# Experts' loads: overflow pairs in reverse order at the same places, and half of one weight set asked for earlier

## Chip, cores and metric

The kernel runs on one core of one Trainium2 chip. The metric is the device time of one execution in microseconds. The median of the timed runs is what counts; the trace comes from one further, profiled execution.

## What is computed

Two transformer blocks in float32 on 512 tokens of width 1024. All that this change touches is the last stage, a mixture of 32 experts, of which each token uses two:

```python
def _hierarchical_moe(xt, w_rg, b_rg, w_re, b_re, w_gate, w_up, w_down):
    ...
    expert_id = g_idx * EXPERTS_PER_GROUP + top_i
    ...
    for e in range(N_EXPERTS):
        he = jax.nn.silu(xt @ w_gate[e]) * (xt @ w_up[e])
        y = y + combine[:, e:e + 1] * (he @ w_down[e])
```

Each of an expert's three matrices (gate and up 1024 x 256, down 256 x 1024) is 1 MiB, that is 1.0486 MB. There are 512 x 2 = 1024 pairs of a token and an expert, so 1024 rows of 4 KiB are gathered for the experts and as many are scattered back.

## The kernel before

**Tiles.** The experts' stage runs over `NP = 24` tiles, numbered n in the order in which TensorE takes them. A tile holds 64 rows for each of two experts (z = 0 and 1). 16 tiles are "main": main tile m serves the first 64 rows of experts 2m and 2m + 1. The other 8, at the places `OVER_AT = (3, 4, 7, 8, 11, 14, 17, 20)`, are "overflow" pairs, for experts with more than 64 rows. The kernel counts at run time how many blocks of 64 rows beyond the first each expert needs, lists them by rising expert, and gives them the ranks 0, 1, 2 and so on. Overflow pair m serves the ranks m (z = 0) and m + 8 (z = 1). `TILE_PAIRS[n]` says which pair stands at place n. In `WROW` stands, for each rank, from which rows of the weights its loads are to read; for a rank that nobody has, the rows lie behind the end of the tensor. There `bounds_check` drops the row: the instruction is issued all the same, but moves no weights.

**Loads.** A main tile's six matrices are asked for on SyncE's queue (`load_gate_up`, L549 and L550, and `load_down`, L556), an overflow tile's on GpSimd (`over_gate_up` and `over_down`, both through `over_rows`, L749). Gate and up weights have three sets of buffers (`GU[n % 3]`), down weights two (`DN[n % 2]`). Tile n's gate and up weights are asked for once TensorE has finished that step of tile n - 3, and SyncE's queue being in order, behind the wait for the down step of tile n - 4. Places 9 and 10 (`HOLD`) hold back their second half until the overflow down weights of tile n - 2 are there.

**Order on TensorE.** Tile n has a gate/up step (L2134, 32 matmuls), a turn of the hidden rows (L2143) and a down step (L2155, 16 matmuls); tile n + 2's gathered rows are turned between them (L2123). TensorE waits ahead of each step for the step's weights. GpSimd also gathers a tile's rows (L741) and scatters its results (L745).

**Start of the stage.** The first four gathers read `xn_d`, a copy of the normed rows in HBM. They wait for its four stores (`d_xn`, on ScalarE's queue) and for the routing on VectorE (`v_sl`).

Of the kernel before, what the change touches and what calls it, by code (L numbers as in the profile page):

```python
# [148 lines left out]
NP = 24  # L149
OVER_AT = (3, 4, 7, 8, 11, 14, 17, 20)  # L150
HOLD = (9, 10)
TILE_PAIRS = [("over", OVER_AT.index(n)) if n in OVER_AT else ("main", n - sum(k < n for k in OVER_AT)) for n in range(NP)]


def loads_through(n, sets):


    return sum(TILE_PAIRS[k][0] == TILE_PAIRS[n][0] for k in range(n % sets, n + 1, sets))

# [13 lines left out]
def build(nc, a, out):  # L173
    with ExitStack() as ctx:
# [314 lines left out]
        def _(sp):  # L489
# [50 lines left out]

            wg, wu, wd = (a[f"w_expert_{s}_2"][0].rearrange("e (p k) c -> e p (k c)", p=P) for s in ("gate", "up", "down"))

            def load_gate_up(n):
                kind, m = TILE_PAIRS[n]
                if kind == "main":
                    for z in range(2):
                        if z == 1 and n in HOLD:
                            sp.wait_ge(o_dn[n % 2], 32 * loads_through(n - 2, 2))
                        sp.dma_start(GU[n % 3][z][:, 0:2048], wg[2 * m + z]).then_inc(w_gu[n % 3], 16)  # L549
                        sp.dma_start(GU[n % 3][z][:, 2048:4096], wu[2 * m + z]).then_inc(w_gu[n % 3], 16)  # L550

            def load_down(n):
                kind, m = TILE_PAIRS[n]
                if kind == "main":
                    for z in range(2):
                        sp.dma_start(DN[n % 2][z], wd[2 * m + z]).then_inc(w_dn[n % 2], 16)  # L556

            sp.wait_ge(p_pv2, 16)
            load_down(0)
            sp.wait_ge(p_w, 24)  # L560
            load_gate_up(0)
            sp.wait_ge(p_o.sem, p_o.through(4))
            load_gate_up(1)
            sp.wait_ge(d_xn, 16 * 4)
            load_gate_up(2)
            sp.wait_ge(p_ss2, 8)
            sp.dma_start(GB[:, :], bass.AP(a["final_norm_2"].tensor, 0, [[0, P], [1, D]])).then_inc(d_fw, 16)
            sp.wait_ge(p_sl, 1)
# [23 lines left out]
        def _(g):  # L592
# [143 lines left out]
            row_at = bass.IndirectOffsetOnAxis  # L736
            column = lambda n: TILE_PAIRS[n][1] + (0 if TILE_PAIRS[n][0] == "main" else 16)

# [8 lines left out]
            def over_rows(n, z, dst, src, done):  # L747
                m = TILE_PAIRS[n][1] + 8 * z
                g.indirect_dma_start(dst, None, src, row_at(ap=WROW[:, m:m + 1], axis=0), bounds_check=NE * P - 1,  # L749
                                     oob_is_err=False).then_inc(done, 16)  # L750

            def over_gate_up(n):
                if TILE_PAIRS[n][0] == "over":
                    if n >= 3:
                        g.wait_ge(m_gu, n - 2)
                    for z in range(2):
                        over_rows(n, z, GU[n % 3][z][:, 0:2048], wgr, o_gu[n % 3])
                        over_rows(n, z, GU[n % 3][z][:, 2048:4096], wur, o_gu[n % 3])
# [1468 lines left out]
```

## Time and profile before

| | |
|---|---|
| median of 3 runs (lowest, highest) | 1625.91 us (1625.78, 1626.94) |
| profiled execution | 1624.51 us, span 1622.7 us |
| mean granted TensorE clock | 0.973 |
| TensorE matmuls busy | 1502.9 us (93%) |
| read from and written to HBM | 266.42 MB and 16.80 MB |
| SyncE's queue q1; GpSimd's queue q0 | 201.93 MB; 24.16 MB |

The span is from the first to the last instruction. A share of DMA is the mean busy share of the core's 16 DMA engines; a share of about 1 says that all of them move data all the time.

### The profile page before, as it was taken

What the parts mean: (1) busy time and instruction counts of PE and PEld (TensorE: products, weight loads), DVE (VectorE), ACT (ScalarE), POOL (GpSimd) and SP (SyncE); (2) the same over time, 40 slices, a digit from 0 to 9 for tenths busy, and PEclk for the clock granted to TensorE, in tenths of its full rate; (3) what the DMA queues carried; (4) which work ended last, traced back from release to release, by engine and by line L of the source; (5) the groups of instructions that cost most, each with busy time, mean ns of one, the idle gap of its engine ahead of it and who ended that gap; (6) DMA issues with size and microseconds to landing.
All of it is one profiled execution on the core that took longest, in us unless ns stands there. A gap on an engine that the chain in (4) does not pass through costs nothing.

```text
span 1622.7 us, 17325 instructions
## 1 busy us (share of the span) xinstructions
PE 1502.9 (93%) x6765; PEld 785.3 (48%) x6765; DVE 522.3 (32%) x1124; ACT 449.6 (28%) x881; POOL 331.1 (20%) x357
## 2 busy tenths in 40 slices
PE   5998989999999989999999899999999499999992
PEld 2676544455675444455675444455455333333330
DVE  1073310656433210666432211122143412111214
ACT  2234322222763241233762110232232101101101
POOL 1010000453000110555000000004422134323312
PEclk9999999999999999999999999999999699999996
DMA  9654113230110212120100123110500779999994
GB/s 353 239 212 170 53 64 144 78 119 37 50 58 1 94 52 78 53 83 21 55 1 1 52 104 104 52 44 29 193 1 27 275 265 414 369 412 398 402 409 177
DMA packets 85128, 232.98 MB, mean 144 GB/s; under 512 B 17026, under 2 KB 24968, under 8 KB 70841
## 3 DMA queue, kind: packets, MB, share of 16 engines
q1 hardware_dynamic: 69426, 201.93, 33.0%
q0 software_dynamic: 13824, 24.16, 4.1%
q10 hardware_dynamic: 1798, 5.80, 0.9%
q8 instruction: 54, 0.88, 0.2%
q14 instruction: 26, 0.21, 0.0%
HBM read 266.42 MB, written 16.80 MB: 175 GB/s over the span
## 4 chain that ended last, share of the span: by engine, by line
PE 88%; DMA 3%; ACT 3%; DVE 3%; issue 2%; POOL 0%; SPq 0%; DVEq 0%; POOLq 0%; ACTq 0%
PE PS L1719 19%; PE PS L2134 10%; PE PS L1887 9%; PE PS L1950 7%; PE PS L2155 5%; PE PS L1799 5%; PE PS L1698 4%; PE PS L1948 3%; PE PS L2043 3%; PE PS L1821 3%; PE PS L1809 2%; PE PS L1761 2%; PE PS L1985 1%; DMA RING<-in_w_mod_dram 1%; PE PS L2012 1%
## 5 line engine op out<-in xcount | busy, mean ns | idle before, releaser
L1719 PE MATMUL PS<-RH,RING 128*128 128x512 f32 (+1 forms) x864 | 315.9, 522 | 2.2 <-DMA RING<-in_w_in_dram 2.2
L1719 PEld LDWEIGHTS PS<-RH,RING 128*128 128x128 f32 x864 | 162.4, 190 | 146.9 <-issue 136.1
L1887 PE MATMUL PS<-RING,RY 128*128 128x512 f32 x320 | 139.5, 593 | 0.0
L2134 PE MATMUL PS<-RING,RM 128*64 128x512 f32 x384 | 116.7, 609 | 8.4 <-issue 5.6
L611 POOL TENSOR_SCALAR SMALL<-SMALL 128x1 f32<-128x1 f32 (+1 forms) x36 | 11.0, 306 | 537.7 <-ACT WS L833 266.1
L1249 DVE SCALAR_TENSOR_TENSOR RM<-RM,COL 128x512 f32<-128x512 f32 (+1 forms) x180 | 115.1, 707 | 0.2
L1950 PE MATMUL PS<-RH,RING 128*128 128x512 f32 x256 | 113.8, 593 | 0.0
L1290 DVE TENSOR_REDUCE SMALL<-PS 128x1 f32<-128x768 f32 (+1 forms) x80 | 68.0, 850 | 136.7 <-PE PS L1799 136.7
L1799 PE MATMUL PS<-RK,RH 96*128 96x256 f32 (+1 forms) x288 | 105.9, 487 | 1.1 <-ACT WS L976 0.7
L1887 PEld LDWEIGHTS PS<-RING,RY 128*128 128x128 f32 x320 | 60.1, 190 | 72.7 <-issue 72.7
L613 POOL TENSOR_TENSOR SMALL<-SMALL 128x1 f32<-128x1 f32 (+2 forms) x58 | 61.6, 1062 | 87.4 <-DVE SMALL L1223 84.4
L2134 PEld LDWEIGHTS PS<-RING,RM 128*64 128x64 f32 x384 | 37.4, 140 | 83.5 <-issue 80.1
L1950 PEld LDWEIGHTS PS<-RH,RING 128*128 128x128 f32 x256 | 47.2, 190 | 55.0 <-issue 55.0
L1121 ACT ACTIVATE RM<-PS 128x256 f32<-128x256 f32 x24 | 9.2, 385 | 221.7 <-PE PS L2134 221.7
L1799 PEld LDWEIGHTS PS<-RK,RH 96*128 96x128 f32 x288 | 49.9, 191 | 41.3 <-issue 39.4
L1698 PE MATMUL PS<-RING,RH 128*128 128x416 f32 (+1 forms) x192 | 62.9, 488 | 4.4 <-ACT RH L845 4.4
L976 ACT ACTIVATE WS<-PS,SMALL 128x768 f32<-128x768 f32 (+1 forms) x80 | 64.9, 812 | 3.0 <-DVE SMALL L1290 2.9
L1809 PE MATMUL PS<-CST,WS 128*128 128x128 f32 x416 | 59.4, 274 | 6.5 <-ACT WS L967 3.5
L1599 DVE TENSOR_TENSOR RM<-RM,PS 128x256 f32<-128x256 f32 x24 | 10.1, 421 | 160.3 <-ACT RM L1121 160.3
L2134 PE MATMUL PS<-RK,RM 128*64 128x512 f32 x128 | 58.6, 612 | 0.0
L1809 PEld LDWEIGHTS PS<-CST,WS 128*128 128x128 f32 x416 | 49.3, 141 | 18.4 <-issue 12.0
L1948 PE MATMUL PS<-RING,RH 128*128 128x512 f32 x128 | 56.4, 596 | 0.0
(336 smaller groups left out, 2251.0 us busy)
## 6 DMA issues: line engine op xcount, KB each, us to landing
RING<-in_w_in_dram SPq DMA_DIRECT2D x18, 2048.0 KB, 8.6
RING<-in_w_mod_dram SPq DMA_DIRECT2D x12, 2048.0 KB, 9.2
RING<-in_w_expert_gate_dram SPq DMA_DIRECT2D x19, 1024.0 KB
RING<-in_w_expert_up_dram SPq DMA_DIRECT2D x19, 1024.0 KB
RING<-in_w_out_dram SPq DMA_DIRECT2D x8, 2048.0 KB, 8.2
RK<-in_w_expert_down_dram SPq DMA_DIRECT2D x8, 1024.0 KB
X<-in_w_expert_down_dram SPq DMA_DIRECT2D x8, 1024.0 KB
WS<-in_w_expert_down_dram SPq DMA_DIRECT2D x8, 1024.0 KB
```

The lines of the kernel that those rows point to most:

```text
L976: A(PR[n % 2][:, 0:nk], src, ACT.Exp, bias=nmx[:, n % 4:n % 4 + 1], accum_out=DEN[:, q % 2, h:h + 1]).then_inc(a_e.sem, 1)
L1249: ins = v.scalar_tensor_tensor(acc, src, w, acc, ALU.mult, ALU.add)
L1290: v.tensor_reduce(nmx[:, n % 4:n % 4 + 1], free(PS[:, 2 * (n % 2), :], [1, nk]), AX, ALU.max, negate=True).then_inc(v_mx.sem, 1)
L1698: last = mm(o[:, 0:width], HT[:, k, t * P:(t + 1) * P], w[:, k, :], start=(k == 0), stop=(k == 7))
L1719: last = mm(o[:, 0:T], w[:, k, m * P:(m + 1) * P], HT[:, k, 0:T], start=(k == 0), stop=(k == 7))
L1799: last = mm(PS[:, 2 * (n % 2) + c0 // 512, 0:w], RHf[0:QK, h * 512 + q * P:h * 512 + (q + 1) * P], KT[0:QK, h, c0:c0 + w], start=True, sto ...
L1809: last = tr(PS[:, 4 + j // 4, (j % 4) * P:(j % 4 + 1) * P], PR[k % 2][:, j * P:(j + 1) * P], IDENT)
L1887: last = mm(PS[:, j % 2, :], YT[:, k, t * P:(t + 1) * P], w[:, k, :], start=(k == 0), stop=(k == 7))
L1948: last = mm(PS[:, w % 2, :], HT[:, k, tile], wt[:, k, :], start=(k == 0), stop=(k == 7))
L1950: last = mm(PS[:, w % 2, :], wt[:, k, tile], HT[:, k, :], start=(k == 0), stop=(k == 7))
L2134: last = mm(PS[64 * z:64 * z + 64, n % 2, :], XGT[n % 2][:, k, 64 * z:64 * z + 64], free(GU[n % 3][z], [2048, 2], [1, DE], off=DE * k), st ...
L2155: last = mm(PS[64 * z:64 * z + 64, 2 + c, :], HET[n % 2][:, j, 64 * z:64 * z + 64], DN[n % 2][z][:, 1024 * j + 512 * c:1024 * j + 512 * c ...
```

## The change

Two lines of the schedule change. The overflow pairs stand at the same eight places, but pair 7 now comes first (n = 3) and pair 0 last (n = 20). And of tile 2's gate and up weights, those of its first expert are now asked for directly behind tile 1's, ahead of the wait for the stores of the normed rows; the second expert's are still behind it.

```diff
-TILE_PAIRS = [("over", OVER_AT.index(n)) if n in OVER_AT else ("main", n - sum(k < n for k in OVER_AT)) for n in range(NP)]
+TILE_PAIRS = [("over", 7 - OVER_AT.index(n)) if n in OVER_AT else ("main", n - sum(k < n for k in OVER_AT)) for n in range(NP)]
...
-            def load_gate_up(n):
+            def load_gate_up(n, experts=(0, 1)):
                 kind, m = TILE_PAIRS[n]
                 if kind == "main":
-                    for z in range(2):
+                    for z in experts:
...
             load_gate_up(1)
+            load_gate_up(2, (0,))
             sp.wait_ge(d_xn, 16 * 4)
-            load_gate_up(2)
+            load_gate_up(2, (1,))
```

No instruction changes its place on any engine; what moves is a wait, and which columns of `WROW` and `SLOT` the overflow tiles' loads, gathers and scatters read. SyncE's queue at the start of the stage, before (RING, RH and RY hold gate and up weights; the first two rows are tile 1's second expert, RH is tile 2's first and RY its second; `normed_rows_stored` is `d_xn`):

```order
L549 DMA RING<-in_w_expert_gate_dram 128x2048
L550 DMA RING<-in_w_expert_up_dram 128x2048
L549 DMA RH<-in_w_expert_gate_dram 128x2048 [waits normed_rows_stored]
L550 DMA RH<-in_w_expert_up_dram 128x2048
L549 DMA RY<-in_w_expert_gate_dram 128x2048
L550 DMA RY<-in_w_expert_up_dram 128x2048
```

And the same place of the changed kernel:

```order
L549 DMA RING<-in_w_expert_gate_dram 128x2048
L550 DMA RING<-in_w_expert_up_dram 128x2048
L549 DMA RH<-in_w_expert_gate_dram 128x2048
L550 DMA RH<-in_w_expert_up_dram 128x2048
L549 DMA RY<-in_w_expert_gate_dram 128x2048 [waits normed_rows_stored]
L550 DMA RY<-in_w_expert_up_dram 128x2048
```

The wait has moved from the first to the second expert of tile 2; all rows keep their places.

## Rows read from the trace of the kernel before

**Rows 1.** The page's DMA queues: packets, MB, share of 16 engines.

```profile
q0 software_dynamic: 13824, 24.16, 4.1%
```

**Rows 2.** The chain that ended last: start us, us, what.

```profile
1376.93 3.58 PE PS L2155 x16
1380.52 1.17 issue
1381.68 7.09 PE PS L2134 x32
...
1393.60 6.87 PE PS L2134 x32
1400.46 0.37 PE PS L2143 x2
1400.83 0.87 PE PS L2123 x8
1401.71 3.58 PE PS L2155 x16
1405.29 0.54 issue
1405.83 7.09 PE PS L2134 x32
...
1417.75 3.88 issue
1421.63 8.78 PE PS L2134 x32
```

**Rows 3.** Windows of the stage: length, busy us of engines, then PEclk, DMA share, GB/s.

```profile
1298.40:1333.80 35.40, 33.99 (x158) 12.66 (x160) 5.74 (x11) 3.07 (x7) 12.36 (x13) 0.94 0.72 266
1333.80:1345.40 11.60, 11.60 (x60) 4.42 (x58) 2.39 (x4) 1.34 (x3) 4.04 (x4) 1.00 0.91 351
1345.40:1380.50 35.10, 35.10 (x176) 13.02 (x172) 7.21 (x12) 4.03 (x9) 16.07 (x16) 1.00 1.02 415
1380.50:1390.00 9.50, 8.33 (x46) 3.77 (x45) 1.11 (x2) 0.75 (x2) 3.01 (x3) 1.00 1.02 407
1390.00:1400.00 10.00, 10.00 (x49) 3.30 (x48) 1.98 (x3) 0.60 (x1) 4.04 (x4) 1.00 0.62 230
1400.00:1490.00 90.00, 85.58 (x420) 33.28 (x416) 17.24 (x29) 10.15 (x23) 30.14 (x30) 0.98 1.02 414
1490.00:1495.00 5.00, 5.00 (x26) 1.78 (x26) 1.98 (x3) 0.60 (x1) 1.02 (x1) 1.00 0.91 317
1495.00:1525.00 30.00, 30.00 (x152) 11.52 (x148) 5.22 (x9) 3.43 (x8) 11.05 (x11) 1.00 1.00 409
1525.00:1535.00 10.00, 10.00 (x48) 3.36 (x48) 1.98 (x3) 0.60 (x1) 2.03 (x2) 1.00 0.93 355
1535.00:1580.00 45.00, 45.00 (x226) 17.38 (x224) 9.61 (x16) 5.37 (x12) 6.00 (x6) 1.00 1.01 414
1580.00:1585.00 5.00, 4.53 (x22) 1.52 (x20) 0.42 (x1) 0.75 (x2) 0.00 (x0) 1.00 0.72 266
1585.00:1590.00 5.00, 4.49 (x22) 1.55 (x20) 0.69 (x1) 1.06 (x3) 0.97 (x1) 1.00 0.03 12
```

**Rows 4.** Windows of three tiles each, and a 5 us one, the same columns.

```profile
1482.01:1517.09 35.08, 35.08 (x176) 13.30 (x174) 7.21 (x12) 4.03 (x9) 12.06 (x13) 1.00 0.99 396
...
1455.00:1460.00 5.00, 5.00 (x25) 1.75 (x26) 1.98 (x3) 0.60 (x1) 1.02 (x1) 1.00 1.02 401
```

**Rows 5.** The timeline of SyncE's queue: start us, us, what is asked for.

```profile
1266.54 0.65 SPq L550 DMA_DIRECT2D RING<-in_w_expert_up_dram  x1
1278.91 0.33 SPq L549 DMA_DIRECT2D RH<-in_w_expert_gate_dram  x1
...
1345.48 0.33 SPq L549 DMA_DIRECT2D RING<-in_w_expert_gate_dram  x1
...
1368.91 0.33 SPq L556 DMA_DIRECT2D RK<-in_w_expert_down_dram  x1
...
1380.59 0.33 SPq L549 DMA_DIRECT2D RING<-in_w_expert_gate_dram  x1
```

**Rows 6.** Windows at the stage's start, columns as in group 3.

```profile
1275.00:1280.00 5.00, 1.70 (x6) 1.46 (x6) 2.97 (x14) 2.61 (x10) 0.00 (x0) 0.50 0.85 326
1280.00:1285.00 5.00, 0.99 (x18) 0.99 (x20) 4.76 (x17) 0.00 (x0) 0.00 (x0) 0.50 0.89 365
1285.00:1290.00 5.00, 0.96 (x18) 0.80 (x16) 1.24 (x7) 0.00 (x0) 2.30 (x2) 0.50 1.02 429
```

**Rows 7.** The chain that ended last, at the stage's start and end.

```profile
1287.19 7.71 DMA RM<-normed_rows,SLOT
1294.90 0.14 issue
...
1587.94 3.67 PE PS L2155 x16
1591.61 0.02 issue
...
1593.16 2.56 DMA pair_rows<-WUKV,SLOT
```

## The prediction

> **What bounds the kernel now.** The change lies in the experts' stage alone, so I read that stage in three views: the chain that ended last, the windows with the DMA share, and the timelines of the two queues that ask for weights.
>
> The chain runs through TensorE without a gap from tile to tile: 6.87 + 0.37 + 0.87 + 3.58 = 11.69 us a tile [rows 2]. It is broken three times, ahead of the gate/up steps of tiles 7, 9 and 10: 1.17, 0.54 and 3.88 us. "issue" there is a wait whose end the profile does not name; the step waits for its rows and its weights, and the DMA engines are full at that time, so I take it for the weights. The steps behind these waits are longer too: 7.09, 7.09 and 8.78 us against 6.87.
>
> The windows say how near the rest of the stage is to the same wait [rows 3]. From 1400 to 1580 us the share is 0.91 to 1.02, mostly 1 and more, at 409 to 414 GB/s. The share falls below 0.95 in only two short places (1490 to 1495 and 1525 to 1535) before the stream ends between 1580 and 1585, 3 to 8 us ahead of the last down step at 1587.94 [rows 7]. So TensorE sets the pace there, and the loads are just behind it, with almost nothing to spare.
>
> **Which overflow pairs are real.** Queue q0 moved 24.16 MB [rows 1]. 2 x 1024 rows of 4 KiB are 8.39 MB of it; the other 15.77 MB are 15.04 matrices, hence five experts with three each. By the code they are ranks 0 to 4, so pairs 0 to 4 load one expert each and pairs 5, 6 and 7 none. The windows agree: they sum to 108.9 MB from 1298.4 on [rows 3]; 82 matrices on SyncE's queue (86.0 MB) and 7.7 MB of rows leave 15.2 MB, where 15 matrices are 15.7.
>
> Before, the real pairs are at places 3, 4, 7, 8 and 11, the empty ones at 14, 17 and 20. Afterwards 3, 4 and 7 are empty, and 8, 11, 14, 17, 20 real. Nine matrices (9.44 MB) thus leave the time before tile 9 and come after tile 12.
>
> **Term 1, the early waits.** With nine matrices less in their way, the weights of tiles 7 and 9 come in time, and probably those of tile 10. Saved: 1.17 + 0.54 + 3.88, and of the steps behind them 0.22 + 0.22 + 1.91: 7.9 us.
>
> **Term 2, the earlier half set.** Two matrices of tile 2 are asked for some 12 us sooner, at about 1267 instead of 1278.9 [rows 5]. They queue behind tile 1's four, so all they can fill are the pauses in the stream, 0.15 and 0.11 of two 5 us windows, 1.3 us in all [rows 6]. Tile 2 never waited. What may gain is the first gather, which took 7.71 us beside these loads, while the last scatter, with an idle stream, took 2.56 [rows 7]. Bounds: 0, and 7.71 - 2.56 = 5.1 us if the stream were empty. It is not: at 1287 it runs at 1.02 and would end 1.3 us sooner. I take 0.7 us. The stores that gate the gathers share the stream with tile 1's loads in both kernels, so I charge nothing; they had landed by 1278.9, 8 us ahead of the gather.
>
> **Term 3, the late waits.** I do this as an account of the stream.
>
> First, where it is caught up. Between 1345.4 and 1380.5 the changed kernel has to load ten matrices: six's four of gate and up, four of down (tiles 5 and 6), and two for overflow tile 8 on q0. SyncE cannot ask for tile 9's before about 1380.6 [rows 5]. Ten matrices at 414 GB/s are 25.3 us and three tiles' rows 2.5 us, 28 of the 35 us. The stream runs dry. The time freed early is not used, since there is no free buffer to load into: this is where the expected gain goes.
>
> Then, what is left. Eleven main tiles of six (9, 10, 12, 13, 15, 16, 18, 19, 21, 22, 23) are 66 matrices, tile 8's down is one, four overflow tiles are 12: 79, or 82.8 MB. Rows: 30 of 48 gathers and scatters, 5.2 MB. Together 88.1 MB, at 414 GB/s 212.8 us. To this I add 3 us for pauses: some 2 us until the first bytes of tile 9 flow (the 2.56 us of the small scatter is the nearest row), and 1 us where `HOLD` keeps back tile 10's second half. The stream then ends at 1380.5 - 0.7 + 3 + 212.8 = 1595.6.
>
> Last, the tie to the end. Before, the mean engine's stream ends at 1580 + 0.72 x 5 + 0.03 x 5 = 1583.8, but some bytes come after 1585 [rows 3], so the slowest DMA engine is at least 1.3 us behind the mean and at most 4.2. I take 3. Tile 23's down step starts at 1598.6 where it was 1587.94 [rows 7]: **+10.7 us**.
>
> The same by difference: before, 9.42 + 4.07 + 14.57 = 28.1 MB of the 109.4 (86.0 + 7.7 + 15.7) were moved by 1380.5, leaving 81.3; afterwards 6.8 MB more are left, 16.4 us. Against it stand the pauses of before that disappear: 3.8 us (1390 to 1400), 0.45 and 0.7, in all 5.0. With 3 us of new pauses and the 0.7 us, the stream ends 13.7 us later than 1583.8, and the down step starts at 1600.5: +12.6. The ways differ because the stretches at 407 and 409 GB/s count as 414 in the first. I take +11.5.
>
> A check by tiles: three tiles with an empty pair take 396 x 35.08 = 13.9 MB [rows 4], 33.6 us at 414 GB/s, 1.5 us less than the three tiles last. With a real pair it is 17.0 MB or 41.2 us, 6.1 us more than 35.08. From tile 8 on five such periods follow; the lead at their start is at most 11 us. So the new waits add up to 11.5 + 7.9 + 0.7 = 20 us, some 3 to 6 us each, once per three tiles from tile 10 to 13 on. The wait of 3.88 us brought a step 1.91 us longer [rows 2]; beside a stream that is the bound this is hidden, save behind the last wait.
>
> **Sum.** -7.9 - 0.7 + 20.1 = +11.5 us. Against the profiled execution (1624.5, a span of 1622.7 and 1.8 around it) that is 1636; that execution was 1.4 us under the median of the runs, so for the median I say 1637.4. What follows tile 23 is unchanged.
>
> The Trainium skill, "DMA: Bandwidth & Descriptors", section Bandwidth, puts the limit of loads from HBM at about 358 GB/s a core. The trace disagrees: 414 GB/s stand for 90 us. By 358 the 88.1 MB would take 246 us, the result would be near 1671, and before would have had to wait in every three tiles.
>
> **Rivals.**
> - *The waits go and do not come back* (the other side): -7.9 - 0.7, hence 1617. For it: three tiles with an empty pair leave a reserve. Against it: to end by 1577 the stream would need 88.1 MB in 195 us, 452 GB/s; the highest row is 429. It decides from a stream that keeps up at 450, or if the early time can be used to load ahead, which the three sets forbid. 0.06.
> - *The stream is slower when never paused*: at the lowest full window, 401 GB/s [rows 4], 219.7 us, 7 more, and the clock behind the last wait 2: +20, 1646. 0.12.
> - *A milder end*: the gather gains its full 5.1 us (4.4 more), or lag and pauses are at their good ends (1.3 us each, 3.4 in all): +3 to +8, 1631. 0.14.
> - *A draw*: stream and waits cancel within 0.2%. It needs three of the bounds at their good ends. 0.04.
>
> **How the numbers follow.** My forecast, +8 to +17, has 0.64. 0.2% (3.3 us) is about what a measurement of this kernel can tell from no change. Slower: 0.64 + 0.12 + 0.13 = 0.89; the same 0.04 and 0.01 of the mild case; faster 0.06. The range takes in the mild and the slow case: 1629 to 1646.
>
> **What would show it.** In the profile of the changed kernel: no wait ahead of tiles 7 and 9; a stream with pauses from 1300 to 1380, below 0.85 on the mean from 1345 to 1380; from about 1385 a share of 1 without a break until about 1595; waits of 3 to 6 us ahead of gate/up steps near tiles 13, 16, 19 and 23; the first gather at about 7 us. I am wrong if the pauses before 1380 don't appear (then the real pairs are elsewhere), if the late share stays below 1, or if the waits come ahead of the turns of gathered rows (L2123): then q0's queue is the bound, not the bytes.

## The result and the profile after

The changed kernel takes 1649.3 us in the median of 4 runs (1648.6 to 1650.7), the kernel before on the same chip 1626.4 us (1625.8 to 1626.9): a ratio of 1.0142 (95% interval 1.013 to 1.0154), so 22.9 us slower. The direction, the mechanism and most places of the waits are as forecast; the size is twice the forecast, and the time lies 3.3 us above the range. The profiled execution took 1648.9 us, with a span of 1647.1 us at a mean granted TensorE clock of 0.966.

The chain of the changed kernel, to be held against [rows 2] (start us, us, what; only the waits and the gate/up steps, L2135 now, behind them):

```profile
1417.36 0.86 issue
1418.22 7.09 PE PS L2135 x32
...
1441.83 1.87 issue
1443.70 7.09 PE PS L2135 x32
...
1455.61 3.63 issue
1459.24 8.44 PE PS L2135 x32
...
1484.21 2.92 issue
1487.13 7.09 PE PS L2135 x32
...
1499.04 3.52 issue
1502.56 8.79 PE PS L2135 x32
...
1527.87 1.72 issue
1529.59 7.09 PE PS L2135 x32
...
1541.50 3.44 issue
1544.94 9.96 PE PS L2135 x32
...
1583.16 7.09 PE PS L2135 x32
...
1595.07 3.60 issue
1598.67 8.71 PE PS L2135 x32
...
1612.76 3.67 PE PS L2156 x16
```

The waits of before at tiles 7 and 9 are gone, and that at tile 10 is 0.86 us. New ones stand ahead of tiles 12, 13, 15, 16, 18, 19 and 23. These seven and that of tile 10 sum to 21.6 us, against 5.6 for the three of before; the steps behind them and that of tile 22 are longer than 6.87 us by 9.5 us in all, against 2.35. The difference, 16.0 + 7.2 = 23.2 us, is the loss as TensorE sees it, from its first gate/up step on.

The windows of the same execution, columns as in [rows 3]:

```profile
1300.20:1335.50 35.30, 33.92 (x158) 12.38 (x156) 5.73 (x10) 3.06 (x7) 11.99 (x13) 0.93 0.41 143
1335.50:1347.20 11.70, 11.70 (x62) 4.43 (x58) 2.40 (x4) 1.34 (x3) 4.03 (x4) 1.00 0.92 350
1347.20:1382.30 35.10, 35.10 (x177) 13.30 (x174) 7.21 (x12) 4.02 (x9) 16.03 (x16) 1.00 0.87 326
1382.30:1395.00 12.70, 12.70 (x64) 4.72 (x62) 3.10 (x5) 1.34 (x3) 4.24 (x5) 1.00 0.66 237
...
1395.00:1515.00 120.00, 107.20 (x514) 41.55 (x512) 20.93 (x35) 12.01 (x27) 35.89 (x36) 0.97 1.02 416
1515.00:1520.00 5.00, 5.00 (x26) 1.71 (x24) 0.69 (x1) 0.10 (x1) 2.41 (x3) 1.00 0.94 365
1520.00:1540.00 20.00, 18.28 (x94) 7.34 (x92) 4.11 (x7) 2.26 (x6) 7.60 (x8) 1.00 1.02 422
1540.00:1565.00 25.00, 21.57 (x92) 7.57 (x90) 3.10 (x5) 1.78 (x4) 4.04 (x4) 0.86 0.97 386
1565.00:1595.00 30.00, 29.99 (x150) 11.96 (x146) 6.52 (x11) 4.04 (x9) 1.98 (x2) 1.00 1.01 417
1595.00:1600.00 5.00, 1.40 (x6) 0.58 (x6) 0.69 (x1) 0.00 (x0) 0.98 (x1) 0.85 0.88 324
1600.00:1605.00 5.00, 5.00 (x20) 1.60 (x18) 0.00 (x0) 0.00 (x0) 0.00 (x0) 0.80 0.63 239
1605.00:1610.00 5.00, 4.53 (x24) 1.46 (x22) 0.42 (x1) 0.76 (x2) 0.00 (x0) 1.00 0.11 46
```

Read the last two columns downwards. Up to 1335 the stream carries 143 GB/s where it carried 266: some four matrices fewer. It still pauses up to 1382 (0.87; the prediction's sign was "below 0.85"), so this time is lost. Between 1382.3 and 1395, where the prediction saw the stream full again from about 1385 on, it is at 0.66. From 1395 to 1540 it is full except for 5 us. From 1382.3 to the end these windows hold 88.4 MB; the account of the prediction had said 88.1.

Two more things differ from before. The chain's first gather is shorter, while the stage begins later:

```profile
1290.47 5.89 DMA RM<-normed_rows,SLOT
```

It took 7.71 us at 1287.19 [rows 7]. And SyncE's queue, ahead of the place where the two programs first differ (start us, us, what is asked for, tile 1's first matrix):

```profile
1268.96 0.33 SPq L549 DMA_DIRECT2D RING<-in_w_expert_gate_dram  x1
```

In the profile of before that request stands at 1265.10. So 3.9 us of the 24.4 us between the two spans lie ahead of the stage. I therefore measure the stage apart, from this request to the end of the span: 357.6 us before, 378.1 us after, +20.5 us. "Stage" means this length from here on.

### The profile page after: what moved, and what is told of

Read it like the earlier page. It is cut to its first block, busy times and chain, and to the rows that moved or that the text cites. A ratio compares the mean times of both kernels' runs of the same rounds, so it can differ in the third digit from the quotient of the medians.

```text
span 1647.1 us, 17325 instructions
## 1 busy us (share of the span) xinstructions
PE 1515.6 (92%) x6765; PEld 790.7 (48%) x6765; DVE 522.3 (32%) x1124; ACT 449.3 (27%) x881; POOL 329.9 (20%) x357
## 3 DMA queue, kind: packets, MB, share of 16 engines
q0 software_dynamic: 13824, 24.16, 3.9%
## 4 chain that ended last, share of the span: by engine, by line
PE 88%; DVE 3%; ACT 3%; issue 3%; DMA 3%; POOL 0%; SPq 0%; DVEq 0%; POOLq 0%; ACTq 0%
PE PS L1720 18%; PE PS L2135 11%; PE PS L1888 8%; PE PS L1951 7%; PE PS L2156 5%; PE PS L1800 5%; PE PS L1699 4%; PE PS L1949 3%; PE PS L2044 3%; PE PS L1822 3%; PE PS L1810 2%; PE PS L1762 2%; PE PS L1986 1%; PE PS L1649 1%; PE PS L2013 1%
## 5 line engine op out<-in xcount | busy, mean ns | idle before, releaser
L2135 PE MATMUL PS<-RING,RM 128*64 128x512 f32 x384 | 121.4, 635 | 20.8 <-issue 18.0
L2135 PEld LDWEIGHTS PS<-RING,RM 128*64 128x64 f32 x384 | 38.9, 146 | 98.9 <-issue 95.4
L2135 PE MATMUL PS<-RH,RM 128*64 128x512 f32 x128 | 57.9, 606 | 3.6 <-issue 3.6
L2135 PE MATMUL PS<-RK,RM 128*64 128x512 f32 x128 | 59.0, 615 | 0.0
```

Of the source, the lines that this page charges most:

```text
L2135: last = mm(PS[64 * z:64 * z + 64, n % 2, :], XGT[n % 2][:, k, 64 * z:64 * z + 64], free(GU[n % 3][z], [2048, 2], [1, DE], off=DE * k), st ...
```

## Experiments

Ratios are to runs of the kernel before on the same chip, with 95% intervals.

**reverse_only** and **early_only** take the change apart: the kernel before with the one line or the other.

```diff
-TILE_PAIRS = [("over", OVER_AT.index(n)) if n in OVER_AT ...
+TILE_PAIRS = [("over", 7 - OVER_AT.index(n)) if n in OVER_AT ...
```

> The overflow pairs in reverse order alone. If the nine matrices that move behind tile 12 carry the loss (my theory), this is slower than before by 23 to 26 us: all of the 22.9 us of the whole change, and the 1 to 2 us that the earlier half set gives back. The stretch ahead of the experts' stage should then stand as in before, or, if the 3.9 us by which the changed kernel is late there belongs to the program and not to the edit, anywhere between 0 and 4 us off. Rival: the earlier half set disturbs something and carries part of the loss; then this one is slower by under 20 us.

Measured: 1648.2 us, ratio 1.014 (1.0122 to 1.0158), stage 377.9 us. The reverse order carries the whole loss: 22.95 us by the medians, at the lower end of what I expected. Its first gather took 8.10 us, and yet its stage is as long as that of the full change with 5.89: the two us that the change gains at the start it loses again in waits and longer steps. The waits fall elsewhere here: the last long one stands ahead of tile 21 (3.80 us), and ahead of tile 23 there is 0.14 us.

> The earlier half set alone, pairs in the old order. My theory: the first gather takes 5.9 us instead of 7.7, the stage starts 1.5 to 2 us sooner, and the time is 0 to 3 us below before (1623 to 1626). Rival: the 3.9 us by which the changed kernel reached the stage late come from this edit; then it is 1 to 3 us slower than before and its trace shows the same 3.9 us at SyncE's first load of tile 1.

Measured: 1625.6 us, ratio 0.9999 (0.999 to 1.0008). The first gather took 6.16 us and the stage 355.4 us; the request for tile 1 came at 1268.97, with the same code ahead of it as in before. That is 3.9 us later than in before, as the rival said, but the time is not the 1 to 3 us longer that it said with it. And the request of reverse_only, which lacks the edit, came late too, at 1268.61. So the late start doesn't come from this edit.

**before_again** is the kernel before once more.

> The kernel before once more, for a second profile. In the first one SyncE asked for tile 1's weights at 1265.1 us; in four other kernels that are the same up to there it was 1267.6 to 1270.1. If that scatter belongs to single executions, this profile lies between 1265 and 1270, and its stage, from that request to the end, takes 357 to 358 us as in the first. If the first lay where this kernel always lies, it is 1265 again.

Measured: the request at 1265.92, a stage of 357.7 us, one run of 1625.4 us. Over all fourteen profiles, all of programs that are the same up to there, the request lies between 1265.1 and 1270.1 us. Four are at 1265.1 to 1265.9 (two of before, two_late, early_no_hold), the others at 1267.6 to 1270.1. Timed runs of before range from 1623.1 to 1630.0 us. So the start scatters; whether it also depends on the program can't be told from one profile each. The early waits scatter too: in this profile they stand ahead of tiles 9 and 10 alone, 2.32 and 4.28 us, where the first had three.

**early_again** repeats early_only.

> The earlier half set alone, a second time. Its first profile had a stage of 355.4 us against 357.6 and 357.7 of two profiles of before, yet the timed runs stood at 0.9999 (0.999 to 1.0008). If the first gather gains 1.5 to 2 us and before's stage can pass it on, this profile again shows a gather near 6 us and a stage of 355 to 356, and the time is 0 to 2 us below before. If the gain is lost in the waits at tiles 9 and 10, the stage is 357 to 358 again.

Measured: ratio 0.9987 (0.9977 to 0.9997), a gather of 6.10 us, again a stage of 355.4 us. The profile's 2.2 us repeat: the first gather takes 5.9 to 6.2 us in all eight profiles with the earlier half set and 7.7 to 8.7 in the six without. The timed difference, 0.0001 and 0.0013 in two tries, isn't clear of the 0.2% that a measurement can tell.

**one_late** and **two_late** are the dose: one or two real pairs are moved behind tile 12 in the kernel before, three in the change. At the eight places stand these pairs:

```diff
-... ("over", OVER_AT.index(n)) ...
+... ("over", (0, 1, 2, 5, 4, 3, 6, 7)[OVER_AT.index(n)]) ...
```

and, for two_late,

```diff
-... ("over", OVER_AT.index(n)) ...
+... ("over", (0, 1, 5, 6, 4, 2, 3, 7)[OVER_AT.index(n)]) ...
```

> Kernel before, with overflow pairs 3 and 5 changed over: place 8 is empty, place 14 loads one expert. Three matrices (3.15 MB, 7.6 us of stream) move late instead of nine. If loss goes with what no longer fits behind tile 12: three tiles with a real pair need 6.1 us more stream than they last, the lead at tile 15 was about 3 us, so a new wait of 3 to 5 us comes there, and of the early 7.9 us some 5 to 8 go: within 4 us of before. Rival: each real pair moved late costs a third of the whole loss, 7 to 8 us.

> Kernel before, with overflow pairs 2 and 3 at places 14 and 17, and empty pairs at 7 and 8. Six matrices (6.3 MB, 15.2 us of stream) move late. With one pair moved the stage grew by 2.5 us: 7.6 us less the 5 us of pauses that before had left in its stream. By the same account two cost 15.2 - 5 = 10 us, plus 0 to 3 for longer steps and new pauses: 1635 to 1639. Rival: the cost grows by a fixed sum for each pair, 20.5 / 3 or some 7 us: 1639 to 1641; or the loss needs all three: under 1633.

Measured: one_late 1.0019 (1.0009 to 1.0028), stage 360.1 us; two_late 1.0053 (1.0035 to 1.007), 1635.4 us, stage 368.2 us. Against the 357.65 us of before, the stage grows by 2.5, 10.5 and, with three (reverse_only), 20.3 us. The loss grows with what is loaded late, and the rival of a fixed 7 us a pair fails at one_late.

My account was 7.6 us of stream a pair at 414 GB/s, less the 5 us of pauses that before had left: 2.6, 10.2 and 17.8. The first two fit, and two_late was a forecast that held (its timed difference, 8.6 us with 5.7 to 11.4, fits too). But the traces do not bear the account out. The same stretch of before, one_late, two_late and reverse_only, in this order, from 115.4 us behind the request for tile 1 (where before asks for tile 9's weights) to the last down step:

```profile
1380.50:1587.94 207.44, 200.87 (x982) 76.57 (x981) 40.24 (x67) 23.23 (x52) 57.29 (x57) 0.99 0.97 390
...
1385.52:1595.46 209.94, 201.93 (x978) 76.65 (x975) 39.59 (x67) 23.20 (x52) 57.12 (x57) 0.98 0.97 389
...
1381.23:1598.94 217.71, 204.04 (x979) 77.54 (x975) 39.81 (x67) 23.22 (x52) 57.11 (x57) 0.98 0.96 385
...
1384.01:1612.26 228.25, 208.19 (x978) 78.83 (x975) 39.78 (x67) 23.28 (x52) 57.25 (x57) 0.96 0.96 388
```

By length times rate that is 80.9, 81.7, 83.8 and 88.6 MB. So 0.8, 2.9 and 7.7 MB more come behind this point, not 3.15, 6.3 and 9.44: 1.9, 7.1 and 18.5 us of stream, where the stretch grows by 2.5, 10.3 and 20.8. And the pauses do not go away: in one_late the stream is at 0.73 from 1380 to 1400, and no wait stands behind that of tile 15. Too many bytes moved and pauses taken for filled made up for each other in the first two; that they agreed was luck.

**after_no_weights** drops the rows of the overflow tiles' weights, which leaves out that part of the computation. Queue q0 then moves 8.46 MB in place of 24.16.

```diff
-... bounds_check=NE * P - 1,
+... bounds_check=0,
```

> The changed kernel, with every row of the overflow tiles' weights dropped by the bounds check: the instructions are issued, but none of the 15.7 MB are moved (the overflow tiles compute with stale weights). If bytes are the bound, no wait ahead of a gate/up step above 0.5 us is left, and the time is that of the changed kernel less 21.6 us of waits and 9.5 us of longer steps, about 1618. Rival: the order of requests on GpSimd's queue or the holds at places 9 and 10 bind; then waits of several us stay, and the time is above 1625.

Measured: 1617.2 us, ratio 0.9945 (0.993 to 0.996), stage 348.8 us. Of the eight waits one is left, ahead of tile 23:

```profile
1567.25 1.73 issue
1568.98 7.10 PE PS L2135 x32
```

That is where three main tiles follow each other, and more than the 0.5 us that I allowed. The instructions and their order are those of the changed kernel: the bytes make the loss, 29.3 us of stage for 15.7 MB.

**after_no_hold** removes the holds at places 9 and 10 from the changed kernel.

```diff
-HOLD = (9, 10)
+HOLD = ()
```

> The changed kernel with HOLD = (), so that tiles 9 and 10 ask for both halves at once. In the changed kernel the second half of tile 9 was asked for 8.4 us behind the first, for down weights of tile 7 that are empty, and the stream paused some 5 us between 1382 and 1395. My theory: every pause of a stream that is the bound costs its length, so this is 3 to 6 us faster than the changed kernel (1643 to 1646). Rival: the pause is covered by the lead, or the overflow loads of tile 8 come later in exchange; then the time is the same within 1.5 us.

The hold of tile 9 in the changed kernel's queue; its first half, then the second (timeline of SyncE's queue):

```profile
1382.73 0.43 SPq L550 DMA_DIRECT2D RING<-in_w_expert_up_dram  x1
1391.59 0.33 SPq L549 DMA_DIRECT2D RK<-in_w_expert_gate_dram  x1
```

and without the hold:

```profile
1382.30 0.43 SPq L550 DMA_DIRECT2D RING<-in_w_expert_up_dram  x1
1382.78 0.43 SPq L549 DMA_DIRECT2D RK<-in_w_expert_gate_dram  x1
```

Measured: 1645.5 us, ratio 1.0118 (1.0101 to 1.0135) against 1.0142 for the changed kernel, so some 3.9 us less, with intervals that just overlap; stage 375.9 us, 2.2 us less. From tile 7's gate/up step to the last down step it is 227.0 us against 230.5; the start and the tail take back 1.2 us of this. Between 1382 and 1395 the stream is at 0.92 instead of 0.66:

```profile
1382.00:1395.00 13.00, 13.00 (x66) 4.86 (x64) 3.00 (x5) 1.34 (x3) 4.68 (x5) 1.00 0.92 348
```

The hold waits for down weights of tile 7 that the reverse order has made empty. It costs some 3 us of stream (0.92 less 0.66, of 13 us) for nothing. On GpSimd's queue of the changed kernel these loads stand from 1383.09 on:

```profile
1383.09 0.99 POOL L750 DMA_INDIRECT WS<-in_w_expert_down_dram,WROW  x1 [2.60 <-PE PS L2156]
```

**before_no_hold** is the same edit on the kernel before.

> The kernel before with HOLD = (). Its stream paused 3.8 us between 1390 and 1400, ahead of the waits of 0.5 and 3.9 us at tiles 9 and 10. If a pause costs its length wherever a wait follows, this is 2 to 5 us faster than before (1621 to 1624). Rival: the overflow weights of tiles 7 and 8 then share the stream with tile 9's second half and come late, and the wait only moves to their steps: within 1.5 us of before.

Measured: ratio 1.0012 (1.0003 to 1.0021), stage 359.0 us. The pause is filled (419 GB/s between 1390 and 1400), but its chain has one long wait in place of those ahead of tiles 7, 9 and 10:

```profile
1402.24 7.94 issue
1410.18 5.50 PE PS L2155 x16
```

L2155 is a down step, that of tile 7, whose overflow weights now share the stream with tile 9's second half. The rival had the mechanism right (its bound of 1.5 us less so, the runs are 2.0 us slower, 0.5 to 3.4): there, a filled pause only moves the wait.

**early_no_hold**, that and the earlier half set.

> The earlier half set, old pair order, HOLD = (). If the two gains add up: 3 to 6 us faster than before (1620 to 1623). Rival: both only feed the same waits at tiles 9 and 10, and the sum is no more than one of them, 0 to 3 us.

Measured: 1.0001 (0.9991 to 1.0011), stage 358.7 us, one wait of 8.14 us at the same place. Nothing is gained.

**one_late_early_no_hold**: the earlier half set, no holds, and the pair order of one_late.

> As the last one, and place 8 empty and place 14 with one expert. The early waits should be gone entirely; the late surplus of 7.6 us of stream meets a lead that starts 3 to 5 us larger. My account: within 3 us of early_no_hold. Rival: as in one_late alone, 2 to 4 us slower than the old order.

Measured: 1624.3 us, ratio 0.9983 (0.9974 to 0.9992), stage 355.2 us. It is 2.8 us faster than before (1.3 to 4.2), the lowest ratio of all versions that compute everything, though still within the 0.2% that I called the bound and not clear of early_again's 0.9987. The account held and the rival fell: it is no slower than early_no_hold. With place 8 empty, the down step of tile 7 no longer waits, and the late surplus costs one wait of 3 us, ahead of tile 13, and two of 1.1 to 1.3 us later:

```profile
1451.84 2.99 issue
```

**after_short_last** cuts the last four matrices, the down weights of tiles 22 and 23, to 64 columns; the rest of them is left out of the computation.

```diff
-sp.dma_start(DN[n % 2][z], wd[2 * m + z]).then_inc(w_dn[n % 2], 16)
+w = 64 if n >= 22 else 2048
+sp.dma_start(DN[n % 2][z][:, 0:w], wd[2 * m + z][:, 0:w]).then_inc(w_dn[n % 2], 16)
```

> The changed kernel with the down weights of tiles 22 and 23 cut to 64 of 2048 columns (the rest of these weights is left out, stale ones are used). 4.1 MB less, 9.8 us of stream at its very end. My prediction tied the end of the stage to the last bytes: then this is 6 to 9 us faster than the changed kernel. The trace says that the last wait is that for tile 23's gate and up weights, asked for ahead of those: then only the two matrices of tile 22 that share the stream with them can matter, and the gain is 0 to 4 us.

Measured: 1647.6 us, ratio 1.0128 (1.0111 to 1.0145), stage 378.8 us against 378.1. 9.8 us less stream at the end give back nothing in the profile, and in the timed runs 0.0014 of the ratio, some 2 us, with intervals that overlap. The wait ahead of tile 23 is as long as ever, and the down steps follow without one for weights:

```profile
1593.95 3.54 issue
1597.49 8.80 PE PS L2136 x32
...
1607.11 3.65 PE PS L2157 x16
...
1611.65 3.67 PE PS L2157 x16
```

(Lines are one further on in this kernel.) The end of the stage hangs on tile 23's gate and up weights here, not on the last bytes. But something else shows, now that almost nothing is asked for behind these weights:

```profile
1585.00:1590.00 5.00, 5.00 (x29) 2.33 (x26) 0.42 (x1) 0.75 (x2) 0.00 (x0) 1.00 0.80 320
...
1590.00:1597.00 7.00, 3.95 (x20) 1.18 (x18) 1.98 (x3) 0.60 (x1) 0.97 (x1) 1.00 0.22 81
```

From 1590 on the mean share is 0.22, and yet the step waits until 1597.49. By the trace's records of single transfers only 65 of the 8 KiB pieces of these weights end behind 1590, 0.53 MB or 1.3 us of a full stream, but the last of them ends at 1596.95. So the load is not even: a few of the 16 DMA engines are some 7 us behind the others, and the step waits for the slowest.

## Why the prediction was wrong

**Right.** That pairs 0 to 4 are the real ones; that the early waits go; that the time freed early is not used, since no buffer is free to load into; that the late tiles wait for bytes, from tile 10 to 13 on (four waits of 3.4 to 3.6 us near tiles 13, 16, 19 and 23 as forecast, but four more of 0.9 to 2.9 that were not); that the remaining load is 88.1 MB at 414 GB/s (88.4 MB measured, full windows 416 to 422). Term 1 was nearly right: 0.86 us of wait and 0.22 of a longer step are left at tile 10, of 7.9 us. The rival on the other side did not occur, and the draw neither; the stream was not slower when never paused.

**Wrong.** Term 3, in its last step, *the tie to the end*, and in a term before it, *3 us for pauses*. Both ways of the account added the same two. The first way gave +10.7 us for the start of tile 23's down step. From the request for tile 1 to that step it is 343.8 us after and 322.8 before, so +21.0. The parts:

- *The tie*: I let the last down step start 3 us behind the mean end of the stream, as if it waited for the last bytes, with 3 us for the slowest DMA engine. The stream ends at 1600 + 0.63 x 5 + 0.11 x 5 = 1603.7, the step starts at 1612.76, 9.1 us later: **+6.1 us**. Two things are in it. The last large transfer ends at 1609.72 by the trace's records, so the slowest engine is 6.0 us behind the mean, not 3; in before it was 2.8 (1586.55 against 1583.8), so my reading of before was good and did not carry over. And the step comes 3.0 us behind even that, since it does not wait for its own weights: the last wait is that for tile 23's gate/up weights, and behind it TensorE still has a gate/up step, a down step and the hand-overs, 14.1 us from 1598.67. after_short_last shows both, the wait that stays without the last bytes and the engines that lag. Why they lag more when the stream is always full stays open. Nor is it always tile 23 that waits: reverse_only loses as much, and its last long wait is at tile 21.
- *The pauses*: 88.4 MB at 414 GB/s are 213.5 us, and took 221.4 from 1382.3. That is 7.9 us of pauses for the 3 I had, **+5.6 us** together with the 0.3 MB. 5.4 us of it lie between 1382.3 and 1395, where tile 9's second half is held; I had counted 2 us there until the first bytes flow and 1 us for the hold of tile 10, and nothing for that of tile 9: an empty transfer also has to be issued and to land before the hold ends. after_no_hold gives 2 to 4 us of it back. The rest are pauses at 1515, at 1540 to 1565 and at the end. There SyncE asks for the next set only behind a down step that itself is late: a stream that is the bound of TensorE is held up by TensorE's lateness. The trace has this for two of them: the request of 1559.76 stands right behind the down step that ends at 1559.72, with a share of 0.50 from 1558.76 to 1560.76, and that of 1595.11 behind the one that ends at 1595.07, with 0.43 from 1595 to 1596. No run takes the order of the queue apart.
- *The start of the stage* gained 2.1 us instead of 0.7: **-1.4 us**. The gather went from 7.71 to 5.89 us; the 1.3 us of pauses that the earlier half set can fill were a poor measure for a gather behind 2 MB of other loads.

10.7 + 6.1 + 5.6 - 1.4 = 21.0.

*The longer steps.* I said that they are hidden beside a stream that is the bound, save the last. They sum to 9.5 us here. Without the holds they sum to 5.8 us (more waits, each at most 2.8 us), with waits of 21.7 us against 21.6; the total falls by 3.6, about what the filled pause gives. This fits what I said, but no run separates the clock from the waits. Only the last one, 1.8 us, stands for certain in the sum, within the tie.

*Timed and profiled.* Within the stage the profiles differ by 20.3 to 20.5 us; the timed difference is 22.9 (21.1 to 25.1), and 22.95 (19.8 to 25.7) for reverse_only. The 2.4 us between them may lie ahead of the stage, where the start scatters by 5 us from one execution to another, but timed runs have no profile, and this is not shown. What decides where the start falls stays open.

## What to carry to other kernels

Moving loads later is not free because the wait that they caused is gone: first sum the bytes that remain behind the point where the buffers are full, divide by the rate of the full windows, and compare with the compute left. Tie the end to the last transfer that something waits for, then add all compute behind it, not to the last byte; and take that transfer's end on the slowest DMA engine, which here was 6 to 7 us behind the mean. A sum that fits two points is not proof of its terms: read the bytes and the pauses themselves in each trace. And ask of each hold or wait on another load's semaphore what it does once that load is empty.

## What was not expected of the hardware

An indirect load whose rows are all dropped still holds a waiter for several us when it is issued late: the down weights of tile 7 were asked for from 1383.1 us on, and the queue that waited for them went on at 1391.6. The DMA engines do not end together: with a share of 0.22 on the mean a step still waited 7 us for the slowest. And the length of a wait doesn't settle how long the step behind it is. In the changed kernel waits up to 2.9 us brought steps of 7.1 us and those of 3.4 us and more steps of 8.4 to 10.0, against 6.87 without a wait. But in one_late 2.0 and 2.3 us already brought 8.8, in early_only 3.0 us only 7.1:

```profile
1444.28 1.97 issue
1446.25 8.78 PE PS L2134 x32
```

```profile
1419.52 3.01 issue
1422.53 7.09 PE PS L2135 x32
```

(The first is one_late, the second early_only.) The granted clock of 1540 to 1565 us was 0.86 on the mean in the changed kernel: 0.50 (1.2 GHz) from 1545 to 1550 and 1.00 (2.4 GHz) from 1555 on; the engine had waited 3.44 us ahead of this step.
